# Reordering the edges of a tuned decoder-layer kernel: block scores spread over a wide product, sample keys first, other orders at the FFN's entry and exit and at the end

## The reference

```python
u = rmsnorm(h); z = u @ w_in                       # queries, three K/V pairs, gates, SSM input
kc = gelu(blocks(k_cmp + pe) @ w1) @ w2            # compressed keys: hidden, then second product
s_c = q @ kc.T * scale + bias                      # scores of the compressed blocks
p_c = masked_softmax(s_c); imp = p_c @ overlap     # importance -> top 16 selected blocks
o = g0 * (p_c @ vc) + g1 * selected(q, ks, vs) + g2 * window(q, kw, vw)
h = h + (mg0 * (o @ w_att_br) + mg1 * (ssm(u) @ w_ssm_br)) @ w_o
f = rmsnorm(h)
h = h + (silu(f @ w_ffn_gate) * (f @ w_ffn_up)) @ w_ffn_down
g = sigmoid(rmsnorm(h) @ w_ple_gate)
y = rmsnorm(h + g * (p @ w_ple))                   # y_prompt (512 x 1024), y_sample (32 x 1024)
```

## Time and profile before

| | |
|---|---|
| time, median of 3 runs | 1093.23 us |
| time of the profiled execution | 1092.62 us |
| its span | 1090.8 us |
| PE busy | 1039.9 us, 95% |
| DVE busy | 647.5 us, 59% |
| ACT busy | 479.3 us, 44% |
| POOL busy | 253.7 us, 23% |
| mean granted TensorE clock | 0.978 of full |
| chain that ended last: PE, DVE, ACT | 85%, 6%, 4% |

### The profile page before, as it was taken

How to read it: one execution, slowest core, us unless ns; L and a number is a source line. 1 busy time by engine, 2 the same in 40 slices (tenths; PEclk the granted TensorE clock), 3 DMA queues, 4 the chain that set the end, 5 groups by cost and what they waited for, 6 DMA issues and landing times.

```text
span 1090.8 us, 20592 instructions
## 1 busy us (share of the span) xinstructions
PE 1039.9 (95%) x8381; PEld 988.3 (91%) x8381; DVE 647.5 (59%) x1323; ACT 479.3 (44%) x884; POOL 253.7 (23%) x131
## 2 busy tenths in 40 slices
PE   5999999999999999988999989999999899999997
PEld 4899999998999976655899989999999899999997
DVE  5897886104432237763486799889889861110643
ACT  5456322345233167865423455545555641222322
POOL 3432422332000001031434500000000044445350
PEclk8999999999999899999999989999999989999998
DMA  9544273866339006247724123333333323233302
GB/s 232 132 112 99 78 236 91 258 197 228 103 69 109 1 1 217 103 136 220 213 82 133 41 57 96 98 98 97 97 109 99 104 68 88 87 93 92 108 9 82
DMA packets 164585, 124.75 MB, mean 114 GB/s; under 512 B 21187, under 2 KB 153771, under 8 KB 162700
## 3 DMA queue, kind: packets, MB, share of 16 engines
q1 hardware_dynamic: 160828, 106.63, 35.7%
q0 software_dynamic: 3456, 16.78, 4.5%
q10 hardware_dynamic: 208, 0.03, 0.0%
HBM read 109.66 MB, written 15.69 MB: 115 GB/s over the span
## 4 chain that ended last, share of the span: by engine, by line
PE 85%; DVE 6%; ACT 4%; issue 2%; DMA 2%; SPq 2%; POOL 0%; ACTq 0%; DVEq 0%
PE pair L2113 12%; PE pair L2115 12%; PE pair L2114 12%; PE pair L2296 10%; PE pair L2298 10%; PE pair L2297 10%; PE pair L2120 3%; PE pair L2466 2%; DVE arena L1424 1%; PE pair L2443 1%; PE pair L2453 1%; DMA ring<-in_w_in 1%; PE pair L2291 1%; DVE arena_r L1424 1%; SPq L693 1%
## 5 line engine op out<-in xcount | busy, mean ns | idle before, releaser
L858 POOL TENSOR_TENSOR ring_r<-ring,ring_r 128x1024 fp32r<-128x1024 f32 (+2 forms) x79 | 189.9, 2406 | 545.5 <-ACT ring_r L972 522.2
L2113 PE MATMUL pair<-arena_r,ring_r 128*128 128x272 f32 (+1 forms) x976 | 285.6, 293 | 8.7 <-POOL ring_r L858 4.9
L2115 PE MATMUL pair<-arena_r,ring_r 128*128 128x272 f32 (+1 forms) x976 | 283.2, 290 | 0.0
L2113 PEld LDWEIGHTS pair<-arena_r,ring_r 128*128 128x128 f32 (+1 forms) x976 | 183.2, 188 | 9.8 <-issue 7.4
L2115 PEld LDWEIGHTS pair<-arena_r,ring_r 128*128 128x128 f32 (+1 forms) x976 | 183.0, 188 | 0.4
L2114 PE MATMUL pair<-uT_r,ring_r 128*128 128x272 f32 (+1 forms) x592 | 170.3, 288 | 0.0
L2114 PE MATMUL pair<-arena_r,ring_r 128*128 128x272 f32 x480 | 139.1, 290 | 0.0
L972 ACT ACTIVATE ring_r<-ring 128x1024 fp32r<-128x1024 f32 (+2 forms) x79 | 80.7, 1024 | 103.0 <-PE pair L2115 80.3
L2114 PEld LDWEIGHTS pair<-uT_r,ring_r 128*128 128x128 f32 (+1 forms) x592 | 110.2, 186 | 0.6
L1424 DVE TENSOR_TENSOR arena<-arena 128x256 f32<-128x256 f32 (+6 forms) x150 | 93.7, 647 | 2.6
L2296 PE MATMUL pair<-arena_r 128*128 128x256 f32 (+2 forms) x324 | 95.1, 294 | 0.0
(11 more groups left out here) (385 smaller groups left out, 2394.0 us busy)
## 6 DMA issues: line engine op xcount, KB each, us to landing
ring<-in_w_in SPq DMA_DIRECT2D x26, 512.0 KB, 4.4
ring<-in_w_ffn_gate SPq DMA_DIRECT2D x21, 512.0 KB, 3.9
ring<-in_w_ffn_up SPq DMA_DIRECT2D x21, 512.0 KB, 3.9
ring<-in_w_ffn_down SPq DMA_DIRECT2D x16, 512.0 KB, 4.2
gate_spill<-arena SPq DMA_DIRECT2D x16, 272.0 KB, 4.7
ring<-in_w_o SPq DMA_DIRECT2D x8, 512.0 KB, 4.1
ring<-in_w_ple_gate SPq DMA_DIRECT2D x8, 512.0 KB, 4.1
arena<-gate_spill SPq DMA_DIRECT2D x2, 1904.0 KB, 11.8
```

The source lines that it names most:

```text
L858: eng.tensor_tensor(ring_r[:, n % RING, 0:slab_size(n)], ring[:, n % RING, 0:slab_size(n)], hi, ALU.subtract).then_inc(S["slab_split"], 1)
L2113: eng.matmul(out, w_hi, x_hi(k)[:, cols], start=n == 0, stop=False)
L2115: ins = eng.matmul(out, w_lo, x_hi(k)[:, cols], start=False, stop=n == len(steps) - 1)
```

## The change

Seven pieces, none of which changes what is computed:

1. `block_scores_prompt` is taken apart. Each of its 32 matmuls stands ahead of one step q of `hidden(6, 0)` and `hidden(6, 1)`; the KV head alternates from step to step.
2. On PE `turn_keys(0)` is moved ahead of the sample's `block_scores`, its waits for the queries behind it, and `turn_keys(2)` ahead of `importance(0)`.
3. Two of the groups of transposed keys (`keys_out(6)`) are copied by VectorE and no longer by ACT.
4. FFN entry: the products start (1,0), (5,0), (1,1), (6,0), (2,0), (7,0), (5,1), (4,0), (3,0) and no longer (1,0), (5,0), (6,0), (2,0), (7,0), (1,1), (4,0), (3,0), (5,1); the norm's sum follows (3,0) and no longer (4,0). X1's low part gets its own tile (the one of `vtok`, once its contents are written out) and is made tile by tile early. The weight parts of blocks 0 and 1 are made earlier on ACT and DVE, X3 and X4 last. ACT copies the first partial result (`first_kept`). The last addition of squares on POOL waits until the low parts of X1 to X4 are done.
5. FFN exit: ACT makes the high parts of the first three down slabs between the middle tiles: the first before them, the second after eight, the third after sixteen.
6. End: the square of a tile is taken before the next sigmoid. 21 transposes (t = 0, 1, 2 and k below 7) stand ahead of the wait for the last tile, then the 3 that need it, then the norm's sums, then t = 3 and 4. DVE and ACT share the scaling of t = 4.
7. The loads of `p_prompt` and `p_sample` move on SP's queue from ahead of the FFN's weights to behind product (5, 21).

The core of the diff:

```diff
-    out = [(1, 0)]
-    for c in range(FC):
-        out += [(5, c), (6, c), (2, c), (7, c)] + [(1, c + 1)] * (c + 1 < FC) + [(4, c), (3, c)]
+    out = [(1, 0), (5, 0), (1, 1), (6, 0), (2, 0), (7, 0), (5, 1), (4, 0), (3, 0)]
+    for c in range(1, FC):
+        out += [] if c == 1 else [(5, c)]
+        out += [(6, c), (2, c), (7, c)] + [(1, c + 1)] * (c + 1 < FC) + [(4, c), (3, c)]
...
                 for q in range(16):
                     o = PITCH[n % 2] * (q % 8) + q // 8
                     x = slice(o, o + cols)
+                    if n == 6:
+                        block_score_prompt(16 * h + q)
                     ins = three_terms(bank(hid % 2)[:, 0:cols], w1_high(kv, q)[:, r], w1_lo[kv][:, q, r], XT_hi[n % 2][:, x], XT_lo[n % 2][:, x], q == 0, q == 15)
...
-            def block_scores_prompt():
-                for i in range(TILES):
-                    for g in range(G):
-                        for kv in range(KV):
-                            r = slice(64 * kv, 64 * kv + 64)
-                            c0 = (G * i + g) * CB_P
-                            ins = eng.matmul(bank(2 + kv)[:, c0:c0 + CB_P], zq[r, g, i * P:(i + 1) * P], kcT_p[r, 0:CB_P], start=True, stop=True)
+            def block_score_prompt(s):
+                i, g, kv = s // (G * KV), s // KV % G, s % KV
+                r = slice(64 * kv, 64 * kv + 64)
+                c0 = (G * i + g) * CB_P
+                ins = eng.matmul(bank(2 + kv)[:, c0:c0 + CB_P], zq[r, g, i * P:(i + 1) * P], kcT_p[r, 0:CB_P], start=True, stop=True)
...
+            turn_keys(0)
+            eng.wait_ge(S["qb_ready"], 2)
+            eng.wait_ge(S["o_taken"], 4)
             block_scores(0)
             block_scores(1)
-            turn_keys(0)
             turn_keys(1)
+            turn_keys(2)
             importance(0)
-            turn_keys(2)
...
-            keys_out(6)
+            tb += 2
+            eng.wait_ge(S["tb_copied"], tb)
             keys_out(7)
...
+            for n, j0 in enumerate((0, 4)):
+                eng.wait_ge(S["tb_copied"], 16 + n)
+                eng.wait_ge(S["tb_done"], 17 + n)
+                eng.tensor_copy(KT[:, 2, j0 * P:(j0 + 4) * P], bank(4 + n)).then_inc(S["tb_copied"], 1)
...
+                if not more:
+                    eng.wait_ge(*product_done(3, FC - 2))
+                    weights_high(first)
...
-                    for m in range(4, 12):
+                    for m in range(4, 8):
                         mid_part(m)
+                    weights_high(first + 1)
+                    for m in range(8, 12):
+                        mid_part(m)
...
             for c in range(KC):
                 name = ("pg", c)
+                if c:
+                    last_square(c - 1)
                 eng.wait_ge(*out_of(name))
                 eng.activation(sig[:, c % 2, :], sig[:, c % 2, :], ACT.Sigmoid).then_inc(S["gate_done"], 1)
                 high_after(name)
-                if c:
-                    last_square(c - 1)
...
+            for t, name in enumerate((("pg", KC - 2), ("ple", KC - 2), ("pg", KC - 1))):
                 eng.wait_ge(*out_of(name))
+                for k in range(KC - 1):
+                    turn_y(t, k)
```

More of the change, by code:

```diff
@@ L472, in w_half_lo @@
         def w_half_lo(c, part):
+            if part == "A11" and c == 1:
+                return ar_r(27136, 1, HALF)[:, 0, :]
             return a11_lo if part == "A11" and c >= 2 else w_half(c, part, w_set_lo)
@@ L1327, in _ @@
                 square(1, k)
[L1328 to L1331, removed]
             keep(0, 0, 1, bank_a[0])
             eng.wait_ge(*done(("wo", KC - 1)))
-            eng.wait_ge(*past("t_new", 14))
+            eng.wait_ge(*past("t_new", 15))
             eng.activation(X3_hi, X3, ACT.Copy).then_inc(S["t_high"], 1)
@@ L1337, in _ @@
             eng.activation(X4_hi, X4, ACT.Copy).then_inc(S["t_high"], 1)
-            for c in range(FC):
+            half_high(1, "A12")
+            half_high(1, "S3")
+            keep(0, 1, 6, bank_a[0])
+            half_high(1, "A22")
+            half_high(1, "S4")
+            keep(0, 2, 7, bank_a[0])
+            keep(1, 0, 1, bank_a[1])
+            half_high(2, "A11")
+            half_high(2, "S1")
+            eng.wait_ge(*product_done(4, 0))
+            eng.activation(mid[:, 0, 0:HT], bank(bank_a[0])[:, 0:HT], ACT.Copy).then_inc(S["first_kept"], 1)
+            half_high(2, "S2")
+            half_high(2, "A12")
+            for h in range(2):
+                eng.wait_ge(*past("norm_sum", 1))
+                ins = eng.activation(rt[:, h * HT:(h + 1) * HT], bank(norm_banks[h])[:, 0:HT], ACT.Sqrt, bias=eps_t[:, :], scale=1.0 / D)
+            ins.then_inc(S["root_done"], 1)
+            keep(1, 1, 6, bank_a[1])
+            half_high(2, "S3")
+            keep(1, 2, 7, bank_a[1])
+            half_high(2, "A22")
+            half_high(2, "S4")
+            keep(2, 0, 1, bank_a[0])
+            silu(0)
+            first = split_index[step_slab("wo", KC - 1)] + 1
+            for c in range(2, FC):
                 s, more = c % 2, c + 1 < FC
-                if c and more:
+                if more:
                     half_high(c + 1, "A11")
-                if c:
-                    silu(c - 1)
+                silu(c - 1)
+                if not more:
+                    eng.wait_ge(*product_done(3, FC - 2))
+                    weights_high(first)
                 keep(c, 1, 6, bank_a[s])
@@ L1356, in _ @@
                 else:
-                    for m in range(4, 12):
+                    for m in range(4, 8):
                         mid_part(m)
[L1359 to L1363, removed]
-            first = split_index[step_slab("wo", KC - 1)] + 1
-            eng.wait_ge(*product_done(3, FC - 2))
-            weights_high(first)
+                    weights_high(first + 1)
+                    for m in range(8, 12):
+                        mid_part(m)
             silu(FC - 1)
@@ L1369, in _ @@
                 mid_part(m)
-            weights_high(first + 1)
+            weights_high(first + 2)
             for m in range(16, FC):
                 mid_part(m)
-            weights_high(first + 2)
             def down_parts(k):
```

206 lines of the change are left out of this document (126 added, 80 removed).

## The result

The changed kernel takes 1113.5 us (median of four runs, 1112.4 to 1116.0), the kernel before 1093.8. The ratio is 1.0185, with a 95% interval of 1.0172 to 1.0197: slower by 1.85%. The prediction was 1088.3 us, with a range of 1077 to 1097.

The account below looks back on a forecast made before the run. TensorE, busy 95% of the span, was taken to bound the kernel through its waits, lower clock and work. Terms 8.4 - 3.9 - 2.4 - 5.6 - 0.8 = -4.3 from 1092.62 gave 1088.3 us, range 1077 to 1097.

Parts of the forecast that it names:

- Block scores: Prompt's block scores spread through `hidden(6)`: 32 insertions cost 15.4 us against 7.0 before, net +8.4 us.
- The clock's loss of 2.6 goes, if it goes: Behind the prompt's block scores: 2.6 us lost to the lower clock would vanish, as wide work surrounds each narrow matmul.
- The price of one insertion: One narrow block-score matmul between wide ones in `hidden(6)`: 0.48 us taken, lower bound 0.12 to 0.22, upper 0.49.
- the second rival: Clock falls inside `hidden(6)`: 96 wide matmuls at half, with some 3 for insertions, add 14, giving 1102 us; chance 0.16.
- Sample keys: Start of the sample's attention: transposes fill the first gap (-1.9), VectorE's copies shorten the second (-2.0); together -3.9 us.
- FFN entry: FFN's first products: waits of 1.0, 2.8, 1.9 ahead of (1,1), (6,0), (7,0), 0.5 for clock, against 8.6: -2.4 us.
- FFN exit: First down slab: TensorE's 4.89 wait for POOL and the lower clock behind it go, 6.9 in all; -5.6 us.
- The 1.3 left standing: Down products: middle tiles' low parts on VectorE late while POOL splits the second slab; half of 2.57 kept as loss.
- End: Final norm and outputs: thin part of the transfer and last tile's tail fall away, norm-root path 0.3 shorter: -0.8 us.
- The loads of p: Loads of `p_prompt` and `p_sample`, needed only behind the `w_ffn_down` products, which hide them: 0 us.

Follow-up runs that it names:

- the run with 128 rows: Changed kernel, block scores still spread one by one, but each KV head's keys lie beside 64 rows of zeros so each score uses all array rows: 1088.5 us.
- run with the copies first: Changed kernel with block scores in one block (1084.5 us), ScalarE's two copies of the first turned keys ahead of the sample's first exponential: 1085.5 us.
- the run with the slab earlier: Changed kernel with block scores in one block (1084.5 us), ScalarE's high part of the third down slab ahead of the last silu: 1080.5 us.
- with all three edits: Changed kernel with 16 two-head block scores (128 rows, 62 columns), first key copies ahead of the exponential, and third down slab's high part earlier: 1078.6 us.

## Why the prediction was wrong

**Block scores: the step that failed** is "The clock's loss of 2.6 goes, if it goes: wide work surrounds each narrow matmul". It let the wide matmuls stand for a dense stretch. Spread like this they are no dense stretch, and the clock fell inside it in place of behind it. The price of one insertion, which the step before worked out, was right: 0.48 forecast, 0.52 measured, and the run with 128 rows shows that 0.3 of it is the change of shape. "TensorEngine Tiling (Array Packing)" of the Trainium skill, section "Key Properties", has a change of tiling mode drain TensorE; the 0.22 without and the 0.52 with a change agree.

What happened is the second rival, to which I gave 0.16 and 1102 us. It was too cheap in its size as well: I let the insertions cost "some 3" more at the lower clock. An insertion takes 0.86 there (1.50 less three wide matmuls of 0.21), 0.34 more than at full clock, so 26 of them cost 9 more, not 3. Of the 21.8 us beyond the forecast for this stretch, 16 are the 26 steps at the lower clock; 3.0 are the loss behind the scores, which the forecast let go and which stayed (up to 407.7); 1.2 are insertions at 0.52 and not 0.48, 1.0 the eight transposes between the two halves, now at the lower clock, and 0.6 the wait ahead of `second(6)`. My own sum had the material for a larger chance: it put 0.48 of stall beside 0.36 of wide work into every step, for 27 us on end, and in the kernel before, a block of 4.3 us had been enough to bring the clock down.

**Sample keys.** Of the two parts one was right (-2.2 against -2.0), one wrong (+0.6 against -1.9). The step "Eight transposes now fill the gap (1.1 of 1.57), and the remaining eight gain most of ..." followed TensorE's list and the waits that were removed from it, but not ScalarE's, where the copies of those transposes stand behind an exponential that depends on the block scores. The run with the copies first gives 2.5, which makes -1.8 against the kernel before: the size was right, the path was not.

**FFN entry.** Right in direction, sized too small: -3.4 against -2.4. I laid VectorE's list out to waits of 1.0, 2.8 and 1.9; they are 0, 2.1 and 0.3. VectorE had its parts of block 1 ready in time. The copy ahead of (7,0) was late, as said. Timelines of PE and ACT:

```profile
668.08 0.36 PE L2371 MATMUL pair<-arena_r,zT_r 128*128 128x272 f32 x1 [0.32 <-issue]
...
667.61 0.38 ACT L1324 ACTIVATE ssm_params<-pair 128x272 f32<-128x272 f32 x1
```

The copy ends at 667.99, 0.09 ahead of the product, and the wait is short only because the two products before it ran largely at the lower clock. In the runs with all rows, with the copies first and with all three edits, where those two ran at full clock, TensorE waits 1.8 there, and 1.9 was forecast.

**FFN exit.** The first wait went as forecast (4.89 to 0). The 1.3 left standing for the collision of POOL and VectorE was mis-sized and on the wrong engine: not VectorE's low parts were late but POOL's third split, 2.8 of wait and the clock behind it. -2.5 in place of -5.6; the run with the slab earlier gives 3.7 more. In the run with the copies first it was VectorE's low parts after all, and 3.2 of wait.

**End.** -1.6 against -0.8, just beyond its range of -1.5. The path to the root of the norm was mis-sized: it got 0.9 shorter (8.04 to 7.15) where I allowed 0.3, and VectorE's addition alone gave 0.6 of it. The outputs behind it gave 0.7. The loads of p cost nothing, as said: from 950 us on TensorE's list has no wait for them.

**What was not in the sum.** 1.5 us between the attention and (1,0), where nothing was changed: the clock is at 0.79 and 0.87 in the windows from 555 to 565 us behind a wait of 2.1 that was there before too, without a fall. It comes with the change: every profile with the rest of the change has it (1.5, and 2.7 and 2.5 in the two with the copies first), that of the spreading alone does not. What sets it off isn't shown. Other stretches with the same matmuls lose 1.3 to 1.6 in some of the experiments and not in others, which blurs all totals by some 2 us.

Without the spreading the sum had been -4.3 - 8.4 = -12.7; that kernel gives -9.1 by the medians (1084.5 against 1093.6).

## What to carry to other kernels

Before small matmuls are put among wide ones, work out one whole step with its stalls and ask what the clock will do inside it, not only behind it: a stall of 0.5 us repeated 32 times cost 16 us by itself and another 16 (26 steps at 1.50 in place of 0.88) through the clock. If they must go there, give them the shape of their neighbours (0.22 in place of 0.52), or bundle them so that more wide work stands between. Here the old block was hard to beat all the same: spread with all rows the scores took 1.1 more than in the block, and only half as many of twice the width took less (2.5). When work is moved ahead of a wait, follow its consumers' lists too: a copy that stands behind the old wait on another engine gives the gain straight back.

## What the runs showed of the hardware

The same instructions lost their clock at 360 us in one kernel and after 365 us in another, and unchanged stretches differed by 1 to 2 us between kernels with the granted clock in them. Gains below 2 us are better read between landmarks than from totals.

GpSimd and VectorE can hold each other up in either direction. Before, POOL's splits at the FFN's exit ran in 2.88 or less, and four of VectorE's low parts beside them took 6.99 (timeline of DVE before):

```profile
870.86 6.99 DVE L1424 TENSOR_TENSOR arena_r<-arena,arena_r 128x544 fp32r<-128x544 f32 x4
```

After, one split took 7.56 beside ten low parts that ran at their usual 0.65. In the run with the copies first VectorE's list had the same lead of 0.54 over the same split (873.03 and 873.57, after 903.30 and 903.84), and the split took 1.89. So the order alone doesn't tell which of the two is held up. "SBUF — State Buffer" of the Trainium skill, section "SBUF: two separate sides", has the two lock each other out of a shared port for a whole instruction; the trace agrees in that one of them stands still, but here POOL stood still over ten instructions in a row.
